# Two RWKV chunks invert their triangular matrices in shared visits, with the first level preset instead of multiplied

## The chip, the cores and the metric

The kernel runs on one core of a Trainium2 chip. The metric is the device time of one launch in microseconds (us); lower is better. All weights start in HBM, so the core reads some 149 MB in one execution.

## The reference

Two transformer blocks over 256 tokens of width 1024, in fp32. The first block has a dilated attention branch and an RWKV-7 branch, merged by gates, then a feed-forward layer; the second has three attention branches, a memory attention and a SwiGLU layer. The change touches only the RWKV-7 branch, which in the reference is a scan over tokens, for 8 heads of width 64:

```python
def step(state, inp):
    r_t, w_t, k_t, v_t, a_t, b_t = inp
    sa = jnp.einsum('bhvk,bhk->bhv', state, a_t)
    state = (state * w_t[:, :, None, :] + sa[..., None] * b_t[:, :, None, :]
             + v_t[..., None] * k_t[:, :, None, :])
    y = jnp.einsum('bhvk,bhk->bhv', state, r_t)
    return state, y
state0 = jnp.zeros((B, RWKV_HEADS, HEAD_DIM, HEAD_DIM), f32)
_, y = lax.scan(step, state0, seq)
```

## The kernel before, in words

**The scan as two chunks.** The 256 tokens are cut into two chunks of 128 (`i` = 0, 1). In a chunk, the tokens' influence on each other is a unit lower triangular 128x128 matrix per head; its inverse is needed. The matrix is cut into two diagonal blocks of 64x64 and the 64x64 block below them (`L21`). `LS` holds the diagonal blocks of all 8 heads, one half of the partitions for each of the two. The inverse of a diagonal block is built by doubling, in six levels `lv` = 0 to 5, from blocks of 1 to blocks of 32: `X` is the inverse so far, kept as `XA` and `XB`, so that each of the two diagonal blocks has it and its transpose. A level has two steps, each of them a visit: **T** multiplies `LS` with `X` on TensorE (PE; 16 products of 64x64x64, lines 1148 and 1151), VectorE (DVE) masks the result out of PSUM into `TL` (line 2851, two instructions, one for each half of the partitions), and **X** multiplies `TL` with `X` (32 products, 24 at level 5, lines 1164 to 1172), which ScalarE (ACT) copies back (through its helper at line 1746) into `XA` and `XB`. At level 0 `X` is a constant identity. After level 5, **S** and **X21** (lines 1183 and 1193, 8 products each) put the block below in place, S read out by DVE and X21 by ACT.

**What stands around the chain.** Ahead of it, `first` makes in four visits the strict products (`LS`, `L21`; lines 1096 and 1099), the received part (`LR`, line 1111) and the keyed parts (`M`, two visits, line 1124). Behind it come `rhs` (line 1214, with 1217 for chunk 1), `u` (1228, 1229) and `y` with the new state `h` (1239 to 1255), and then `normed(i)`, the group norm of a chunk. Chunk 1 goes through `first` and the chain only when chunk 0 has gone all the way to its state.

**The order of the work.** Nothing schedules at run time. Each engine's program is a set of Python generators that run in lockstep; a `yield` ends a *visit*. `turns.mix(fills(), rwkv(), order_1())` interleaves two of them by a string: `m` is a visit of the main work, `s` one of the RWKV side. Main work, which I call *fill*, is the block's input projection: `feature_chunk` for the q and k columns (12 products of 128x128x256 a visit, fp32 weights split in a high and a low part, lines 797, 798, 806) and then `token_range` for the gates (six products of 128x128x512, lines 714 to 716 in `mm3`, a visit). The gates' visits run beside those of `attention` (scores at line 1275, softmax on DVE at 2918 and 2505, its transposes at 720, its output at 1318). `rotate` (line 759) is the rotary embedding of q and k. RWKV's products take PSUM banks 4 to 7 in turn; a bank is free for its next user when the event listed in `free` has come.

**Split.** Each weight slot (1 MB) is split by ACT (1746) and DVE (2574), two instructions each, before PE uses it; three slots take turns.

Of the kernel before, what the change touches and what calls it, by code (L numbers as in the profile page):

```python
# [9 lines left out]
F32R = mybir.dt.float32r  # L10
ALU = mybir.AluOpType
# [32 lines left out]
def shape_constants():  # L44
# [12 lines left out]
    for n in range(7):  # L57
        b = 1 << n
        m = (r // (2 * b) == s // (2 * b)) & (r // b % 2 == 1) & (s // b % 2 == 0)
        if n == 0:  # L60
            c[:, C_M0:C_M0 + 128] = m | (r == s)
        else:
            c[:, C_LV + 128 * (n - 1):C_LV + 128 * n] = m | (r == s)
# [79 lines left out]
class Blank:  # L143
# [13 lines left out]
    tensor_tensor_reduce = max = match_replace = dma_start = matmul  # L157
# [117 lines left out]
def program(nc, A, consts, vecs, pt, out):  # L275
    with ExitStack() as ctx:
# [102 lines left out]
        LS, L21, XA, XB, TL, UA = [view(P + o, 512) for o in (15360, 15872, 17408, 17920, 18432, 19968)]  # L379
# [4 lines left out]
        LS4, L214 = [x.rearrange("p (c w t) -> p c w t", c=4, w=2) for x in (LS, L21)]  # L384
# [163 lines left out]
        def order_1():  # L548
            return itertools.chain("msmsm" * 12, "msmsmsm" * 5, "ms" * 35, "mssss", itertools.cycle("ms"))
# [151 lines left out]
        def tensor_program(e, turns):  # L701
# [291 lines left out]
            def rwkv():  # L993
# [88 lines left out]
                for i in range(2):  # L1082
                    def parts(src, p):
                        return v42(src)[half_rows[p], :, i, :]

                    def first():


                        q.wait_ge(*rw_dve.at("ar", 3))
                        q.wait_ge(*rw_dve.at("b"))  # L1090
                        bs = [next(rw_bank) for _ in range(2)]
                        os_ = [bank(b) for b in bs]
                        for c in range(4):
                            for g in range(2):
                                for p in range(2):
                                    mm(os_[p][half_rows[1 - g], 64 * c:64 * c + 64], parts(A4, p)[:, c, half_rows[g]],
                                       AR[half_rows[p], c, i, 0, half_rows[g]], True, True)
                            for p in range(2):
                                t = mm(os_[p][half_rows[1], 256 + 64 * c:256 + 64 * c + 64], AR[half_rows[p], c, i, 0, half_rows[1]],
                                       parts(A4, p)[:, c, half_rows[0]], True, True)  # L1100
                                if c == 3:
                                    t.then_inc(rw_pe.up("LS", i, p), 1)
                        for p in range(2):
                            free[bs[p]] = [rw_dve.at("L21", i, p)]
                        yield
                        bs = [next(rw_bank) for _ in range(2)]
                        os_ = [bank(b) for b in bs]
                        q.wait_ge(*rw_dve.at("r", 3))
                        for c in range(4):
                            for p in range(2):  # L1110
                                t = mm(os_[p][:, 128 * c:128 * c + 128], parts(A4, p)[:, c, :], AR[half_rows[p], c, i, 1, :], True, True)
                                if c == 3:
                                    t.then_inc(rw_pe.up("LR", i, p), 1)
                        for p in range(2):
                            free[bs[p]] = [rw_dve.at("LR", i, p)]
                        yield
                        q.wait_ge(*rw_dve.at("kt"))
                        for h in range(2):
                            bs = [next(rw_bank) for _ in range(2)]
                            os_ = [bank(b) for b in bs]  # L1120
                            for j in range(2):
                                c = 2 * h + j
                                for p in range(2):
                                    t = mm(os_[p][:, 256 * j:256 * j + 256], parts(KM, p)[:, c, :],
                                           AR[half_rows[p], c, i, :, :].rearrange("p w t -> p (w t)"), True, True)
                                    if j == 1:
                                        t.then_inc(rw_pe.up("M", i, p, h), 1)
                            for p in range(2):
                                free[bs[p]] = [rw_dve.at("M", i, p, h)]
                            yield  # L1130

                    def chain():


                        eye = [const(C_D64, 128)[half_rows[g], 64:128] for g in range(2)]
                        lower, upper = half_rows[1], half_rows[0]
                        for lv in range(6):
                            bs = [next(rw_bank) for _ in range(2)]
                            oA, oB = [bank(b) for b in bs]
                            if lv == 0:  # L1140
                                for p in range(2):
                                    q.wait_ge(*rw_dve.at("ls", i, p))
                            else:
                                for g in range(2):
                                    q.wait_ge(*rw_act.at("x", i, lv - 1, g))
                            for h in range(8):
                                s = slice(64 * h, 64 * h + 64)
# [6 lines left out]
                            for g in range(2):  # L1154
                                free[bs[g]] = [rw_dve.at("T", i, lv, g)]
                            yield
                            bs = [next(rw_bank) for _ in range(2)]
                            oA, oB = [bank(b) for b in bs]
                            for g in range(2):
                                q.wait_ge(*rw_dve.at("T", i, lv, g))  # L1160
                            for h in range(8):
                                s = slice(64 * h, 64 * h + 64)
                                xa, xb = (XA[upper, s], XB[lower, s]) if lv else eye
                                mm(oA[upper, s], TL[upper, s], xa, True, True)
                                t = mm(oB[lower, s], TL[lower, s], xb, True, True)
                                if lv == 5 and h == 7:
                                    t.then_inc(rw_pe.up("X", i, lv, 1), 1)
                                t = mm(oA[lower, s], xa, TL[upper, s], True, True)
                                if h == 7:
                                    t.then_inc(rw_pe.up("X", i, lv, 0), 1)  # L1170
                                if lv < 5:
                                    t = mm(oB[upper, s], xb, TL[lower, s], True, True)
# [4 lines left out]
                            yield  # L1177
                        b = next(rw_bank)
                        o = bank(b)
                        q.wait_ge(*rw_act.at("x", i, 5, 1))  # L1180
                        for h in range(8):
                            s = slice(64 * h, 64 * h + 64)
                            t = mm(o[lower, s], L21[lower, s], XB[lower, s], True, True)
# [2609 lines left out]
```

## Time and profile before

| | before |
|---|---|
| median of 3 runs | 940.78 us (940.57 to 940.81) |
| span of the profiled execution | 938.8 us |
| what lies around the span (median less span) | 2.0 us |
| PE busy | 917.2 us, 98% of the span |
| DVE, ACT, POOL busy | 598.4, 446.8, 43.9 us |
| granted TensorE clock | nine tenths or more in each slice |

No time of its own is recorded for the profiled execution beside its span; it is compared with the median of the runs. The two RWKV chunks' chains, with what feeds them, lie between about 87 and 251 us of the span. A product of two fp32 matrices shows in the trace as two instructions, so 16 products are 32 rows. PE's ends are modelled: consecutive starts tell the rate, not the durations.

### The profile page before, as it was taken

What the parts mean: (1) busy time and instruction counts of PE and PEld (TensorE: products, weight loads), DVE (VectorE), ACT (ScalarE), POOL (GpSimd) and SP (SyncE); (2) the same over time, 40 slices, a digit from 0 to 9 for tenths busy, and PEclk for the clock granted to TensorE, in tenths of its full rate; (3) what the DMA queues carried; (4) which work ended last, traced back from release to release, by engine and by line L of the source; (5) the groups of instructions that cost most, each with busy time, mean ns of one, the idle gap of its engine ahead of it and who ended that gap; (6) DMA issues with size and microseconds to landing.
All of it is one profiled execution on the core that took longest, in us unless ns stands there. A gap on an engine that the chain in (4) does not pass through costs nothing.

```text
span 938.8 us, 15782 instructions
## 1 busy us (share of the span) xinstructions
PE 917.2 (98%) x6760; PEld 771.0 (82%) x6760; DVE 598.4 (64%) x952; ACT 446.8 (48%) x722; POOL 43.9 (5%) x60
## 2 busy tenths in 40 slices
PE   7999999999999999999999999999999999999997
PEld 5999887777889988888889988776778798888885
DVE  4668755764684566655765567877772456666773
ACT  4773344255542444445652446483531345455571
POOL 0010000100000000000000350000000000000000
PEclk9999999999999999999999999999999999999999
DMA  9544332222466766555356774343446556665531
GB/s 331 180 134 137 123 104 91 61 77 91 178 231 206 218 185 196 200 181 184 129 180 156 159 242 138 114 169 123 162 151 199 133 163 192 189 180 181 192 121 45
DMA packets 131205, 150.79 MB, mean 161 GB/s; under 512 B 11808, under 2 KB 102176, under 8 KB 131008
## 3 DMA queue, kind: packets, MB, share of 16 engines
q1 hardware_dynamic: 129920, 145.57, 49.7%
q10 hardware_dynamic: 1216, 4.23, 1.2%
q8 instruction: 53, 0.87, 0.4%
q14 instruction: 16, 0.13, 0.0%
HBM read 148.73 MB, written 1.05 MB: 160 GB/s over the span
## 4 chain that ended last, share of the span: by engine, by line
PE 89%; DVE 6%; ACT 2%; issue 2%; DMA 1%; POOL 0%; POOLq 0%; ACTq 0%
PE psum L825 11%; PE psum L714 9%; PE psum L716 9%; PE psum L715 8%; PE psum L826 6%; PE psum L777 6%; PE psum L797 4%; PE psum L798 4%; PE psum L806 4%; PE psum L720 3%; PE psum L873 3%; PE psum L883 2%; PE psum L874 2%; PE psum L828 2%; PE psum L1643 1%
## 5 line engine op out<-in xcount | busy, mean ns | idle before, releaser
L1746 ACT ACTIVATE parts<-low 128x1024 fp32r<-128x1024 f32 (+3 forms) x246 | 248.6, 1044 | 82.4 <-PE psum L716 60.5
L2574 DVE TENSOR_TENSOR parts<-low,parts 128x1024 fp32r<-128x1024 f32 (+3 forms) x150 | 181.3, 1235 | 22.9 <-ACT parts L1746 22.5
L714 PE MATMUL psum<-parts 128*128 128x512 f32 (+2 forms) x424 | 170.1, 401 | 1.0 <-DVE parts L2574 1.0
L716 PE MATMUL psum<-parts 128*128 128x512 f32 (+2 forms) x424 | 163.6, 386 | 0.0
L715 PE MATMUL psum<-parts 128*128 128x512 f32 (+2 forms) x424 | 163.4, 385 | 0.0
L825 PE MATMUL psum<-parts 128*128 128x512 f32 x434 | 155.6, 398 | 0.0
L1746 ACT ACTIVATE high<-psum 128x512 f32<-128x512 f32 (+4 forms) x102 | 55.8, 564 | 161.7 <-PE psum L828 73.1
L826 PE MATMUL psum<-parts 128*128 128x256 f32 x496 | 129.1, 281 | 0.0
L826 PEld LDWEIGHTS psum<-parts 128*128 128x128 f32 x496 | 93.6, 189 | 5.7
L714 PEld LDWEIGHTS psum<-parts 128*128 128x128 f32 x424 | 79.6, 188 | 21.2 <-issue 2.7
L825 PEld LDWEIGHTS psum<-parts 128*128 128x128 f32 x434 | 81.7, 188 | 16.9
L716 PEld LDWEIGHTS psum<-parts 128*128 128x128 f32 x424 | 79.6, 188 | 16.3
L715 PEld LDWEIGHTS psum<-parts 128*128 128x128 f32 x424 | 79.8, 188 | 14.3 <-issue 0.5
L2637 DVE TENSOR_TENSOR parts<-low,parts 128x1024 fp32r<-128x1024 f32 x54 | 66.0, 1223 | 35.2 <-ACT parts L1746 35.2
L797 PE MATMUL psum<-parts 128*128 128x256 f32 (+2 forms) x296 | 78.0, 299 | 0.0
L798 PE MATMUL psum<-parts 128*128 128x256 f32 (+2 forms) x296 | 73.0, 282 | 0.0
L797 PEld LDWEIGHTS psum<-parts 128*128 128x128 f32 (+2 forms) x296 | 55.7, 188 | 4.1 <-issue 2.9
L777 PE MATMUL psum<-low 128*128 128x128 f32 x512 | 58.2, 275 | 0.4 <-DVE low L2551 0.4
L777 PEld LDWEIGHTS psum<-low 128*128 128x128 f32 x512 | 57.8, 192 | 0.8 <-issue 0.6
L798 PEld LDWEIGHTS psum<-parts 128*128 128x128 f32 (+2 forms) x296 | 55.9, 189 | 1.3 <-issue 1.3
L3031 DVE TENSOR_TENSOR mid<-psum,high 128x512 f32<-128x512 f32 x31 | 21.4, 692 | 44.7 <-ACT high L1746 44.7
L806 PE MATMUL psum<-parts 128*128 128x256 f32 (+2 forms) x296 | 41.4, 282 | 0.0
(318 smaller groups left out, 1356.4 us busy)
## 6 DMA issues: line engine op xcount, KB each, us to landing
low<-in_w_in_dram SPq DMA_DIRECT2D x40, 1024.0 KB, 5.2
low<-in_w_ffn_in_dram SPq DMA_DIRECT2D x44, 512.0 KB, 5.2
low<-in_w_ff_in_dram SPq DMA_DIRECT2D x16, 1024.0 KB, 5.6
low<-in_w_ff_out_dram SPq DMA_DIRECT2D x16, 1024.0 KB, 4.9
low<-in_w_ffn_out_dram SPq DMA_DIRECT2D x11, 1024.0 KB, 5.0
low<-in_w_out_dram SPq DMA_DIRECT2D x8, 1024.0 KB, 5.2
low<-in_w_ple_gate_dram SPq DMA_DIRECT2D x4, 1024.0 KB, 4.9
low<-consts_dram ACTq DMA_DIRECT2D x1, 2142.0 KB, 9.1
```

Source lines behind the costliest of these rows:

```text
L714: mm(o, l[0], r[0], start, False)
L715: mm(o, l[0], r[1], False, False)
L716: return mm(o, l[1], r[0], False, stop)
L777: t = mm(PSUM[0:m, banks[n], 256 * j + 128 * i:256 * j + 128 * i + 128], w3[:, k, off:off + m], uT[:, k, 128 * i:128 * i + 128], k == 0, k ...
L797: mm(o, hi[:, k, c], st.uh[:, k, :], k == 0, False)
L798: mm(o, lo_[:, k, c], st.uh[:, k, :], False, False)
L806: t = mm(o, hi[:, k, c], st.ul[:, k, :], False, k == 7)
L825: mm(p, hi[:, k, c], st.u2(k), k == 0, False)
L826: mm(p[:, 0:256], lo_[:, k, c], st.uh[:, k, :], False, False)
L1746: return e.activation(o, a, ACT.Copy)
L2574: tt(rslot3(n, nk, width)[:, r, 0:w], slot3(n, nk, width)[:, r, 0:w], st.hi3(j)[:, r, 0:w].bitcast(F32), ALU.subtract) \
L2637: tt(rview(OR + 2048 * n + 1024 * (k % 2), 1024), slot(n)[:, 1024 * (k % 2):1024 * (k % 2) + 1024], rview(base, 1024).bitcast(F32), ALU.su ...
```

## The change

Both chunks take each step in the same visit. Every tile of the chain (`LS`, `L21`, `XA`, `XB`, `TL`, `UA`) gets a second copy. In T, chunk 0's products go to the upper and lower halves as before and chunk 1's to the opposite halves of the same two banks, so that one visit holds 32 products. X's visit holds chunk 0's 32 products and then chunk 1's. S and X21 are shared too. Level 0 is no longer multiplied: `strict` computes the 64x64 blocks both ways round (64 products in one visit), ACT presets `LS`, `XA` and `XB` of both chunks with identities (six new copies), and DVE writes the strict triangle and the first subdiagonal over them with `COPY_PREDICATED` (12 instructions, where `first` had 12 of other kinds), then the transposed first superdiagonal with four multiplications by a mask. The block below is made by its own 16 products, at level 4. Chunk 0's received and keyed products and masks move into the T visits of levels 1 to 3; chunk 1's come after chunk 0's state. `order_1` gives the side fewer turns and the fill more.

```diff
-            return itertools.chain("msmsm" * 12, "msmsmsm" * 5, "ms" * 35, "mssss", itertools.cycle("ms"))
+            return itertools.chain("msmsm" * 12, "msmsmms", "mms" * 10, "ms" * 4, "mms" * 7, "ms", "mms" * 6, "m" * 14, itertools.cycle("ms"))
...
+                def strict():
+
+                    q.wait_ge(*rw_dve.at("ar", 3))
+                    q.wait_ge(*rw_dve.at("b"))
+                    bs = [[next(rw_bank) for _ in range(2)] for _ in range(2)]
+                    os_ = [[bank(b) for b in x] for x in bs]
+                    for i in range(2):
+                        for c in range(4):
+                            for w in range(2):
+                                for g in range(2):
+                                    for p in range(2):
+                                        l, r = parts(A4, p, i)[:, c, half_rows[g]], AR[half_rows[p], c, i, 0, half_rows[g]]
+                                        if w:
+                                            l, r = r, l
+                                        o = 256 * w + 64 * c
+                                        t = mm(os_[i][p][half_rows[1 - g], o:o + 64], l, r, True, True)
...
-                        for lv in range(6):
+                    for lv in range(1, 6):
                         bs = [next(rw_bank) for _ in range(2)]
-                        oA, oB = [bank(b) for b in bs]
+                        oL, oU = [bank(b) for b in bs]
...
-                                t = mm(oA[upper, s], LS[lower, s], XA[lower, s] if lv else eye[1], True, True)
+                            for i in range(2):
+                                t = mm(oL[half_rows[i], s], LS[i][lower, s], XA[i][lower, s], True, True)
...
-                                t = mm(oB[lower, s], LS[upper, s], XB[upper, s] if lv else eye[0], True, True)
+                                t = mm(oU[half_rows[1 - i], s], LS[i][upper, s], XB[i][upper, s], True, True)
...
+                            free[bs[g]] = [rw_dve.at("T", i, lv, g) for i in range(2)]
+                        if lv == 1:
+                            received(0)
+                        elif lv < 4:
+                            keyed(0, lv - 2)
+                        elif lv == 4:
+                            below()
                         yield
+                        for i in range(2):
...
+                    for h in range(8):
+                        s = slice(64 * h, 64 * h + 64)
+                        for i in range(2):
+                            t = mm(o[half_rows[1 - i], s], L21[i][lower, s], XB[i][lower, s], True, True)
+                    t.then_inc(rw_pe.up("S"), 1)
...
+                yield from strict()
+                yield from turned()
+                yield from chain()
+                yield from state(0)
+                yield from turns.paired(second(), normed(0))
...
+                def eye(name, i, x):
+                    copy(h8(x), rep(const(C_D64 + 64, 64), 8)).then_inc(rw_act.up("eye", name, i), 1)
...
+                    for i in range(2):
+                        for p in range(2):
+                            o = bank(next(rw_bank))
+                            q.wait_ge(*rw_pe.at("LS", i, p))
+                            e.copy_predicated(LS4[i][:, :, p, :], rep(below, 4).bitcast(I32), quarters(o[:, 0:256])).then_inc(rw_dve.up("ls", i, p), 1)
+                            for n, (x, r) in enumerate(((XA4[i], lower), (XB4[i], upper))):
+                                e.copy_predicated(x[r, :, p, :], rep(first_sub[r], 4).bitcast(I32), quarters(o[r, 256:512])) \
+                                    .then_inc(rw_dve.up("xl", i, p, n), 1)
+                    for i in range(2):
+                        q.wait_ge(*rw_dve.at("ls", i, 1))
+                        for g, (x, r, w) in enumerate(((XA[i], lower, upper), (XB[i], upper, lower))):
+                            tt(h8(x[w]), h8(LS[i][r]), rep(first_sup[r], 8), ALU.mult).then_inc(rw_dve.up("xu", i, g), 1)
```

Counted over PE's program from the strict products to the last gate product, the fill of 288 and 192 products in `feature_chunk` and `mm3`, with the 72 of the up projections behind it, stands in 48 pieces before and in 39 after; a piece is fill that nothing else interrupts.

PE, at the end of the first T visit. Before, it holds lines 1148 and 1151, for one chunk, and fill follows (lines 797 to 806):

```order
L1151 MATMUL psum<-low,high 64x64
L1148 MATMUL psum<-low,high 64x64
L1151 MATMUL psum<-low,high 64x64
L797 MATMUL psum<-parts 128x256
L798 MATMUL psum<-parts 128x256
```

Now lines 1165 and 1168 hold both chunks (chunk 1's `XA` lies in `mid`), line 1118 is `received`, and lines 800 and 801 are the fill:

```order
L1168 MATMUL psum<-high 64x64
L1165 MATMUL psum<-mid,high 64x64
L1168 MATMUL psum<-high 64x64
L1118 MATMUL psum<-high 128x128 x8
L800 MATMUL psum<-parts 128x256
L801 MATMUL psum<-parts 128x256
```

The received products, which had a visit of their own ahead of the chain, now stand behind the two chunks' T products.

DVE, after the strict products, now. Lines 2901 and 2903 are the predicated copies, 2908 the superdiagonals, 2747, 2714 and 2753 the rotary embedding, 2643 a slot's split, 2939 the masks of T (before: 2851), 2915 the mask of `received`:

```order
L2903 COPY_PREDICATED mid<-low,psum 64x4x64
L2903 COPY_PREDICATED high<-low,psum 64x4x64
L2908 TENSOR_TENSOR high<-high,low 64x512 x2
L2908 TENSOR_TENSOR mid<-high,low 64x512
L2908 TENSOR_TENSOR high<-high,low 64x512
L2747 TENSOR_TENSOR mid<-psum,low 128x512
L2714 TENSOR_TENSOR mid<-psum,low 128x512
L2753 TENSOR_TENSOR mid<-mid 128x512
L2643 TENSOR_TENSOR parts<-low,parts 128x1024 x2
L2747 TENSOR_TENSOR mid<-psum,low 128x512
L2939 TENSOR_TENSOR high<-psum,low 64x512 x4
L2915 TENSOR_TENSOR high<-psum,low 128x4x128 x2
```

All that `strict` gives DVE now stands in one run ahead of the next slot's split, and the first four T masks come behind that split.

DVE at the third attention block's softmax (lines 2918, 2925 and 2505). Before, T's masks (2851), two operations of `normed(0)` (2816, 2818) and a split (2574) stand between its maxima and its scaling:

```order
L2918 ISA low 128x1
L2851 TENSOR_TENSOR high<-psum,low 64x512 x2
L2816 TENSOR_TENSOR high<-high 128x4x128
L2818 TENSOR_TENSOR high<-high 128x4x128
L2574 TENSOR_TENSOR parts<-low,parts 128x1024
L2925 RECIPROCAL low<-low 128x1
L2505 TENSOR_SCALAR mid<-mid,low 128x768
```

Now it is `rhs`'s copy for chunk 1 (2961), a variance (2873, and a small 2574) and the split (2643), ahead of the scaling (3030, 2574):

```order
L3023 ISA low 128x1
L2961 COPY high<-psum 128x512
L2873 TENSOR_REDUCE low<-high 128x8
L2574 TENSOR_SCALAR low<-low 128x8
L2643 TENSOR_TENSOR parts<-low,parts 128x1024
L3030 RECIPROCAL low<-low 128x1
L2574 TENSOR_SCALAR mid<-mid,low 128x768
```

The chain's masks are gone from the last three softmaxes: the chain is over before the second attention block.

## Rows read from the trace of the kernel before

**Rows 1.** The page: span, busy time of each engine, granted clock in 40 slices.

```profile
span 938.8 us, 15782 instructions
PE 917.2 (98%) x6760; PEld 771.0 (82%) x6760; DVE 598.4 (64%) x952; ACT 446.8 (48%) x722; POOL 43.9 (5%) x60
PEclk9999999999999999999999999999999999999999
```

**Rows 2.** Windows: length, busy us of each engine, clock, DMA share, GB/s.

```profile
110.00:145.00 35.00, 34.77 (x649) 30.86 (x649) 20.92 (x26) 12.92 (x20) 0.00 (x0) 1.00 0.30 92
145.00:172.00 27.00, 25.98 (x366) 20.58 (x365) 12.95 (x22) 9.80 (x17) 0.00 (x0) 1.00 0.26 79
172.00:251.00 79.00, 74.33 (x1132) 58.49 (x1129) 48.55 (x87) 39.29 (x69) 3.88 (x2) 1.00 0.28 95
```

**Rows 3.** Timeline of PE, a T visit, `rotate`, an X visit: start, duration.

```profile
110.76 0.27 PE L1148 MATMUL psum<-low,high 64*64 64x64 f32 x1
...
110.86 0.22 PE L1148 MATMUL psum<-low,high 64*64 64x64 f32 x1
...
110.92 0.22 PE L1148 MATMUL psum<-low,high 64*64 64x64 f32 x1
...
111.83 0.39 PE L797 MATMUL psum<-parts 128*128 128x256 f32 x1
...
114.81 1.02 PE L759 MATMUL psum<-mid,low 128*128 128x512 f32 x2
115.77 0.27 PE L1164 MATMUL psum<-low,high 64*64 64x64 f32 x1
...
116.86 0.38 PE L797 MATMUL psum<-parts 128*128 128x256 f32 x1
```

**Rows 4.** The chain of waits, 90 to 250 us: start, us, what.

```profile
97.78 0.31 PE psum L797
...
99.39 1.06 PE psum L1124 x8
...
157.74 1.14 PE psum L1193 x16
158.88 0.43 PE psum L714
159.54 0.24 PE psum L716
160.47 0.33 PE psum L720 x3
160.80 1.08 PE psum L1214 x32
161.88 0.43 PE psum L714
```

**Rows 5.** Timeline of DVE during the third attention block.

```profile
193.10 0.69 DVE L2918 CUSTOM_DVE_ANT_0 mid<-psum,low 128x512 f32<-128x512 f32 x1 [3.70 <-PE psum L1275]
...
195.39 1.40 DVE L2851 TENSOR_TENSOR high<-psum,low 64x512 f32<-64x512 f32 x2
196.82 0.69 DVE L2816 TENSOR_TENSOR high<-high 128x512 f32<-128x512 f32 x1
...
198.16 1.22 DVE L2574 TENSOR_TENSOR parts<-low,parts 128x1024 fp32r<-128x1024 f32 x1
199.29 0.15 DVE L2925 RECIPROCAL low<-low 128x1 f32<-128x1 f32 x1
199.48 0.62 DVE L2505 TENSOR_SCALAR mid<-mid,low 128x768 f32<-128x768 f32 x1
```

**Rows 6.** Timeline of PE in the same block; in brackets its idle time.

```profile
196.94 0.24 PE L1164 MATMUL psum<-high 64*64 64x64 f32 x1 [1.10 <-DVE high L2851]
```

**Rows 7.** Groups by line and shape, DVE: count, busy us, mean ns, idle.

```profile
L2851 DVE TENSOR_TENSOR high<-psum,low 64x512 f32<-64x512 f32 x24 | 16.5, 688 | 12.9 <-PE psum L1151 12.5
L2826 DVE TENSOR_TENSOR high<-psum,low 128x256 f32<-128x256 f32 x4 | 1.7, 425 | 2.3 <-PE psum L1099 2.2
L2714 DVE TENSOR_TENSOR_SCAN high<-high 128x1024 f32<-128x1024 f32 x1 | 2.3, 2284 | 0.0
```

**Rows 8.** Timeline of ACT after the strict products' operands; in brackets its idle time.

```profile
85.96 2.00 ACT L1746 ACTIVATE parts<-low 128x1024 fp32r<-128x1024 f32 x2
94.42 0.60 ACT L1746 ACTIVATE mid<-psum 128x512 f32<-128x512 f32 x1 [6.46 <-PE psum L806]
```

**Rows 9.** Timeline of DVE: the first mask of `first`, chunk 0.

```profile
92.78 0.42 DVE L2826 TENSOR_TENSOR high<-psum,low 128x256 f32<-128x256 f32 x1 [2.19 <-PE psum L1099]
```

**Rows 10.** Groups by line and shape, ACT, 80 to 250 us.

```profile
L1746 ACT ACTIVATE high<-psum 128x512 f32<-128x512 f32 x26 | 14.4, 596 | 29.3 <-PE psum L1172 18.8 <-PE psum L1244 6.9 <-PE psum L720 3.6
```

More of the change, by code:

```diff
@@ L1194, in chain @@
[L1194 to L1203 removed]
+                    for h in range(8):
+                        s = slice(64 * h, 64 * h + 64)
+                        for i in range(2):
+                            t = mm(o[half_rows[i], s], XA[i][lower, s], TL[i][lower, s], True, True)
@@ L2819, in normed, with strict @@
                     yield
-                for i in range(2):
-                    def first():
+                upper, lower = half_rows
+                def strict():
+                    below, first_sub, first_sup = [const(o, 64) for o in (C_D64, C_M0, C_M0 + 64)]
+                    for name in ("A", "B", "S"):
+                        for i in range(2):
+                            q.wait_ge(*rw_act.at("eye", name, i))
+                    for i in range(2):
                         for p in range(2):
@@ new lines, in strict, with received, keyed @@
+                    yield
+                def received(i):
+                    for p in range(2):
+                        o = bank(next(rw_bank))
+                        q.wait_ge(*rw_pe.at("LR", i, p))
+                        tt(LR4[:, :, p, :], quarters(o), rep(const(C_IU, 128), 4), ALU.mult).then_inc(rw_dve.up("LR", i, p), 1)
+                def keyed(i, h):
+                    msk = const(C_SU, 256).unsqueeze(1).broadcast_to([128, 2, 256])
+                    for p in range(2):
+                        o = bank(next(rw_bank))
+                        q.wait_ge(*rw_pe.at("M", i, p, h))
+                        tt(halves(MN[p][:, 512 * h:512 * h + 512]), halves(o), msk, ALU.mult).then_inc(rw_dve.up("M", i, p, h), 1)
@@ L2862, in rwkv @@
-                    if i == 0:
-                        yield from first()
-                        yield from turned()
-                        yield from chain()
-                    else:
-                        yield from turns.paired(itertools.chain(first(), chain()), normed(0))
+                    o = bank(next(rw_bank))
+                    q.wait_ge(*rw_pe.at("S"))
+                    for i in range(2):
+                        e.tensor_copy(TL[i][lower], o[half_rows[1 - i]]).then_inc(rw_dve.up("S", i), 1)
@@ L2885, in rwkv, with second @@
                     yield
+                def second():
+                    received(1)
+                    keyed(1, 0)
+                    yield
+                    keyed(1, 1)
+                    yield
+                    yield from state(1)
+                yield from strict()
+                yield from turned()
+                yield from chain()
+                yield from state(0)
+                yield from turns.paired(second(), normed(0))
                 yield from normed(1)
```

336 lines of the change are left out of this document (173 added, 163 removed).

## The prediction

> **What bounds the kernel now.** I read the page first: PE is busy for 98% of the span and no other engine for more than 64%, at the full granted clock throughout [rows 1]. So PE's own time sets the end, and a change counts by the PE time that it takes away and by the gaps that it closes or opens. The windows over the stretch of the two chains show those gaps: PE idles for 35.00 − 34.77 = 0.2 us, 1.0 us and 4.7 us in three windows, 5.9 us in all [rows 2]. DVE, at 50 to 60% there, is the engine behind most of them. Everything behind 251 us is untouched, and what is won before it should move the rest forward as it stands.
>
> **How small products are paid.** The timeline of PE gives a price for a visit, not for a product. A T visit (16 products, 32 instructions) starts at 110.76 and the next work at 111.83: 1.07 us. An X visit has twice as many and takes 115.77 to 116.86: 1.09 us [rows 3]. Successive instructions of one line start 0.06 us apart (110.86, 110.92). T's two lines use two 64x64 quarters of the array and X's four lines all four, so a visit costs 16 steps of 0.059 us, 0.94 us, and 0.14 us to get going, however many quarters work. X21, 16 instructions in one quarter, takes 1.14 us in the chain of waits (157.74 to 158.88) [rows 4]. T therefore leaves half of the array empty, S and X21 three quarters; that is what sharing visits can use.
>
> **The change, part by part** (PE, us).
> - T: 12 visits at 1.07 become 5, with 64 instructions on four quarters as X has: 5 x 1.09 = 5.45 for 12.84. −7.4, of which level 0 is 2.1.
> - X: its quarters are full already, so pairing saves only the start: a pair is 32 steps, 1.89 + 0.14 = 2.03. Five pairs are 10.15 for 12 x 1.09 = 13.08. −2.9, of which level 0 is 2.2.
> - S and X21: four visits at 1.07 (1.14 less the overlap with the next work) become two. −2.1.
> - `strict`: 128 instructions on four quarters are 32 steps, 2.03, for two `first` visits at 1.08: −0.1. The block below: 8 steps and a start, +0.6. The received and keyed products keep their number and, having another shape, their start. Together +0.5.
> - Fill restarts: the first instruction of a piece takes 0.43 us in the chain where a later one takes 0.24 (158.88, 159.54), and 0.31 for a 256-column one that then runs at 0.12. That is 0.2 a piece, and there are 39 pieces for 48: −1.8.
> - Gaps. Two of 1.1 us (one shown) stand in front of X in the third and fourth attention block: T's masks end late on DVE behind four softmax instructions [rows 5, 6]. The chain is over by then in the new order, and these and the chain's other waits go. Before X there are now about 5.2 us of PE work (received or keyed 1.07, a piece of fill 1.6 (97.78 to 99.39) [rows 4], `rotate` 0.96 (114.81 to 115.77) [rows 3], another 1.6) where one piece stood; the four masks take 4 x 0.7 = 2.8 us [rows 7]. Before the next T there are 3.0 us of fill, for four ACT copies of 0.6 us [rows 10] of which two are left when X ends. What stays late is the softmax: in the third block DVE has maxima 2.3, a copy 0.7, a variance 0.9, a split 1.2 and a scaling 0.8, 5.9 us, and PE has 2.0 + 3.0 = 5.0 us in between, so about 1 us of idleness. In the fourth PE has 3.4 us and DVE 3.1 plus ACT's exponential between them: 0.2. At the first T masks (next paragraph) about 0.3. 1.5 us for 5.9: −4.4, of which I take 4.0 since the other transposes of attention may wait too.
>
> **DVE after the strict products.** The trace has no predicated copy. Its cheapest price is that of the multiplication it replaces, 0.43 us for 256 columns [rows 7]. The dearest is the slowest streaming instruction in the trace, the scan with 2284 ns for 1024 columns, 0.57 for 256 and with 0.15 of fixed cost about 0.75 us [rows 7]. It is a masked copy of the same shape as the multiplication, so I take 0.45. Then the 12 copies and four superdiagonals occupy DVE from 92.8, when the first products are there [rows 9], for 5.4 + 2.8 us to 101.0; three rotary operations at 0.7 and the split of the next slot (two at 1.2) end near 105.5. On PE `strict` ends at 93.6, and two long pieces of fill (3.0 each), a short one (1.5), `rotate` and eight transposes (0.8) put the first T at 102.9 and the end of its visit at 105.0. The next fill needs that split's second half about 105.9, and X needs the four masks at 105.0 + 1.6 + 0.96 + 1.6 = 109.1, when DVE ends them (a rotary operation 0.7 and 4 x 0.7 behind 105.5) at about 109.0. So this fits with less than 0.5 us to spare, and the cover is PE's own fill. At 0.75 each, DVE is 3.6 us later and PE waits for about 3.5: that is the upper bound. Nothing cheaper than 0.43 is in sight for the shape, and a cheaper one would gain nothing, the work being hidden. The six identity copies on ACT (6 x 0.6 = 3.6 us) fall into its 6.46 us of idleness between 88 and 94.4 [rows 8] and are in front of one split only, whose slot is not read for another 5 us. Without that cover they would be worth the 3.6. In all other places DVE and ACT have about as much to do as before: 20 T masks for 24, four more copies for the block below.
>
> **The sum.** −7.4 − 2.9 − 2.1 + 0.5 − 1.8 − 4.0 = −17.7. The profiled span of 938.8 becomes 921.1; with the 2.0 between span and median, 923.1. The median of the runs shown is 940.78, and I give 923.
>
> **A rule against it.** The rows show that two column halves over the same rows run side by side: `rhs`, 32 instructions of 128 rows by 64 columns, takes 1.08 us (160.80 to 161.88) [rows 4], and X's four quarters 1.09. The Trainium skill (TensorE: Matmul & The Clock Gate, Part 3: Packing small matmuls) says that weight loads overlap running products only when the row group differs. By that rule S and X21, whose two chunks share the lower rows, would stay at two times 16 steps each. The trace does not agree for pairs of other shapes. This gives one of the rivals below.
>
> **The rivals.**
> - *Quarters do not share.* For it: chunk 0's and 1's products in T, S and X21 share row halves, and no row shows just this pairing. Against it: the rows above. Price: T 5 x 0.94 = 4.7 and S and X21 1.9, so 923.1 + 6.6 = 929.7. If only S and X21 fail, by the skill's rule, 925.0. Chance 0.05.
> - *DVE falls behind.* For it: predicated copies near the upper bound, or masks, rotary operations and split in one in-order queue, with a bank that X's first half now gets only when both chunks' masks are done. Against it: DVE is busy 60% there [rows 2]. Price: 3.5 at the start, 1 to 4 more in later levels and softmaxes: 926 to 931, about 928. Chance 0.15.
> - *More is won*: no gap stays and the softmaxes fit too: 918 to 920. Chance 0.06.
> - *Nothing comes out*: the fill, now denser, waits for its weights and gives the time back: about 940. Against it: the DMA share is 0.3 [rows 2]. Chance 0.02.
> - *Slower*: a predicated copy that takes several passes. With some 0.5 us to spare, each further 0.1 us on the 12 costs 1.2; at 1.9 us each the loss is 17 and the gain is gone, and at 2.2 us the time is 923 + 12 x 1.75 − 0.5 = 943.5. No row has anything like it: it would be 8 ns a column against the scan's 2.2. Chance 0.02.
> - *As forecast*: 920 to 926. Chance 0.70.
>
> **Numbers.** The likeliest case gives 923. The range from 918.5 to 929.5 takes in the forecast, most of the extra gain, the upper bound of the predicated copy and most of the lag of DVE; about 0.1 is left out on each side or less. What this measurement can tell from no change is 0.2%, 1.9 us. Faster takes in all cases but two: 0.96; same 0.02; slower 0.02.
>
> **What the changed profile would show.** PE's instructions fewer by 128; T visits of 64 instructions with the next work 1.09 us after their start, X pairs 2.03 us, S and X21 1.07 each; COPY_PREDICATED at about 0.45; PE's idleness from 87 us to the last gate product 1 to 3 us; the up projections about 18 us earlier, and every later stage as long as it was. I am wrong if T takes 2 us, if a predicated copy takes over 0.75, if a gap opens in front of the first two X pairs, or if the saved time reappears as waits for splits in the gates' last seven visits, which now stand in one piece.

## The result, and the profile after

The changed kernel takes 926.12 us (median of four, 924.88 to 926.23) against 940.67 us for the kernel before, measured beside it (940.29 to 940.81). The ratio is 0.9844, with a 95% interval of 0.9832 to 0.9855: faster by 14.6 us. The forecast was 923.0 with a range of 918.5 to 929.5. The profiled execution took 926.23 us, 924.4 of it span, so its span is 14.4 us shorter than that in [rows 1]. One execution of one experiment below, the wait put back, took 1119.87 us at a mean granted clock of 0.75 and counts in no median.

The page and the windows of the changed kernel (columns as in [rows 2]; the last window holds the up products and the transposes behind them):

```profile
span 924.4 us, 15532 instructions
PE 903.4 (98%) x6632; PEld 761.9 (82%) x6632; DVE 598.1 (65%) x956; ACT 447.6 (48%) x724; POOL 44.4 (5%) x61
```

```profile
110.00:145.00 35.00, 34.89 (x844) 31.28 (x845) 27.33 (x39) 15.29 (x25) 0.00 (x0) 1.00 0.29 93
145.00:172.00 27.00, 26.22 (x407) 21.30 (x407) 15.33 (x25) 12.55 (x22) 0.00 (x0) 1.00 0.25 79
172.00:234.00 62.00, 59.01 (x580) 47.20 (x579) 37.75 (x70) 29.91 (x53) 5.03 (x2) 0.97 0.33 105
234.00:256.00 22.00, 20.29 (x92) 15.72 (x91) 19.53 (x25) 11.92 (x17) 0.00 (x0) 1.00 0.57 209
```

PE has 128 instructions fewer and is still what sets the end. Its idle time is not gone: 0.11, 0.78, 2.99 and 1.71 us in these windows, and 5.74 us from 87 to 270 us where the kernel before had 6.28 in the same stretch. One granted clock is no longer 1.00: 0.97 between 172 and 234 us.

The timeline of PE shows the new visits; the start of a visit and the start of the work behind it are what to compare with [rows 3, 4]: the first T visit with the received products behind it, an X pair, S, X21.

```profile
102.52 0.27 PE L1165 MATMUL psum<-high 64*64 64x64 f32 x1
...
103.61 1.16 PE L1118 MATMUL psum<-high 64*128 64x128 f32 x16
104.70 0.38 PE L800 MATMUL psum<-parts 128*128 128x256 f32 x1
...
120.16 0.27 PE L1190 MATMUL psum<-high 64*64 64x64 f32 x1
...
122.19 0.39 PE L800 MATMUL psum<-parts 128*128 128x256 f32 x1
...
159.29 0.27 PE L1212 MATMUL psum<-high 64*64 64x64 f32 x1
...
160.37 0.50 PE L717 MATMUL psum<-parts 128*128 128x512 f32 x1
...
162.28 0.27 PE L1224 MATMUL psum<-high 64*64 64x64 f32 x1
...
163.36 0.50 PE L717 MATMUL psum<-parts 128*128 128x512 f32 x1
```

T with 64 instructions takes 1.09 us, the X pair 2.03, S and X21 1.08 each.

The predicated copies, one line of DVE's queue by source line (in ns: shortest, median, longest):

```profile
L2903 DVE COPY_PREDICATED high<-low,psum x6: 436/444/452, 93.2 to 97.5; 64x256 f32<-64x256 int32 x6
L2901 DVE COPY_PREDICATED high<-low,psum x4: 426/429/445, 92.7 to 96.6; 128x256 f32<-128x256 int32 x4
```

What PE waited for from 87 to 256 us (total us, times, longest), in the view of the waits:

```profile
PE psum L723 <- DVE low L3023: 2.4, 1, 2.4
PE psum L723 <- DVE mid L2577: 0.9, 1, 0.9
PE psum L1315 <- DVE mid L2753: 0.8, 1, 0.8
PE psum L723 <- DVE mid L2574: 0.6, 1, 0.6
PE psum L1378 <- ACT mid L1782: 0.4, 1, 0.4
PE psum L876 <- ACT parts L1782: 0.3, 1, 0.3
PE psum L1190 <- DVE high L2915: 0.2, 1, 0.2
```

The waits in front of X are gone, all but 0.2 us. The two largest waits are new. The largest stands in front of the four transposes of `normed(0)`; this is PE's timeline around it:

```profile
209.06 1.67 PE L1315 MATMUL psum<-mid 64*128 64x256 f32 x12
213.08 0.72 PE L723 MATMUL psum<-low,high 128*128 128x128 f32 x4 [2.35 <-DVE low L3023]
213.50 0.73 PE L717 MATMUL psum<-parts 128*128 128x512 f32 x1
214.03 0.63 PE L718 MATMUL psum<-parts 128*128 128x512 f32 x1
214.46 0.63 PE L719 MATMUL psum<-parts 128*128 128x512 f32 x1
...
216.59 0.57 PE L718 MATMUL psum<-parts 128*128 128x512 f32 x1
217.00 0.39 PE L719 MATMUL psum<-parts 128*128 128x512 f32 x1
```

L3023 is the softmax's maximum over the scores. The transposes read nothing of it. What they share with it is PSUM bank 4: RWKV's ring is (4, 5, 6, 7), attention's is (2, 3, 4), and in the new order the ring of RWKV comes to 4 just when the scores of the fourth attention block (209.06) have taken it. And there is a second cost: behind the wait, products of 512 columns start 0.43 us apart (214.03, 214.46) instead of 0.23 (217.00 and the next, at 217.23). In windows of 2 us the granted clock reads:

```profile
210.00:212.00 2.00, 0.73 (x7) 0.33 (x4) 1.30 (x5) 0.08 (x1) 0.00 (x0) 1.00 0.82 212
212.00:214.00 2.00, 0.92 (x5) 0.86 (x6) 1.73 (x6) 1.89 (x5) 0.00 (x0) 0.89 0.81 312
214.00:216.00 2.00, 2.00 (x6) 1.58 (x5) 0.79 (x2) 2.00 (x7) 0.00 (x0) 0.50 0.00 0
216.00:218.00 2.00, 2.00 (x8) 1.50 (x8) 1.54 (x2) 1.38 (x2) 0.00 (x0) 0.76 0.00 0
218.00:220.00 2.00, 2.00 (x14) 1.70 (x13) 1.97 (x3) 1.36 (x3) 0.00 (x0) 1.00 0.00 0
```

A clock of 0.50 is the 1.2 GHz level. Between 213.50 and 217.00 eight products were started in 3.50 us. At 0.23 apart, with 0.08 more for the first, they need 1.9, so the slow clock cost 1.6 us.

The second largest wait stands behind the up products, in front of the next transposes:

```profile
253.73 1.06 PE L723 MATMUL psum<-low,high 128*128 128x128 f32 x8 [0.87 <-DVE mid L2577]
255.14 0.47 PE L876 MATMUL psum<-parts 128*128 128x512 f32 x1 [0.34 <-ACT parts L1782]
```

The kernel before has only the 0.34 there. By the program this is a shared bank again: these transposes take banks 5 and 6, and in the new order the fourth and last of RWKV's up products has bank 5, which they can have only when DVE has read it (L2577).

The idle time and the slow clock leave the work. The span fell by 14.4, idleness by 0.5, and the slow clock added 1.6, so PE's own work fell by 15.5 us.

### The profile page after: what moved, and what is told of

Read it like the earlier page. It is cut to its first block, busy times and chain, and to the rows that moved or that the text cites. A ratio compares the mean times of both kernels' runs of the same rounds, so it can differ in the third digit from the quotient of the medians.

```text
span 924.4 us, 15532 instructions
## 1 busy us (share of the span) xinstructions
PE 903.4 (98%) x6632; PEld 761.9 (82%) x6632; DVE 598.1 (65%) x956; ACT 447.6 (48%) x724; POOL 44.4 (5%) x61
## 4 chain that ended last, share of the span: by engine, by line
PE 87%; DVE 7%; ACT 2%; issue 2%; DMA 1%; POOL 0%; POOLq 0%; ACTq 0%; DVEq 0%
PE psum L828 11%; PE psum L717 9%; PE psum L718 9%; PE psum L719 9%; PE psum L829 6%; PE psum L780 6%; PE psum L800 4%; PE psum L801 3%; PE psum L809 3%; PE psum L723 3%; PE psum L876 3%; PE psum L877 2%; PE psum L886 2%; PE psum L831 2%; PE psum L1683 1%
## 5 line engine op out<-in xcount | busy, mean ns | idle before, releaser
L1786 ACT ACTIVATE high<-psum 128x512 f32<-128x512 f32 (+5 forms) x93 | 51.3, 563 | 150.6 <-PE psum L831 72.7
L800 PE MATMUL psum<-parts 128*128 128x256 f32 (+2 forms) x296 | 78.8, 302 | 0.0
L801 PE MATMUL psum<-parts 128*128 128x256 f32 (+2 forms) x296 | 72.8, 282 | 0.0
L3580 POOL TENSOR_TENSOR low<-low 128x1 f32<-128x1 f32 x20 | 11.0, 552 | 640.0 <-DVE low L2574 563.3
```

The lines of the kernel that those rows point to most:

```text
L800: mm(o, hi[:, k, c], st.uh[:, k, :], k == 0, False)
L801: mm(o, lo_[:, k, c], st.uh[:, k, :], False, False)
L1786: return e.activation(o, a, ACT.Copy)
```

## The experiments

Each was timed in rounds with the kernel before, whose median was 940.58 to 940.77 in all of them. Differences between two experiments are differences of their medians. In code, PE's program is shown; ACT and DVE are changed to match.

**Level 0 alone** (on the kernel before). In PE's chain:

```diff
-for lv in range(6):
+yield
+yield
+for lv in range(1, 6):
...
-    t = mm(oA[upper, s], LS[lower, s], XA[lower, s] if lv else eye[1], True, True)
+    t = mm(oA[upper, s], LS[lower, s], XA[lower, s] if lv > 1 else eye[1], True, True)
```

> The kernel before, without level 0 of each chunk's chain: its T and X visits, their masks and copies are left out and level 1 starts from the identity, while the two turns stay, empty (so the chain's result isn't the inverse, and the output isn't the reference's). It prices level 0 alone. Theory: each chunk loses a T visit (1.07 us), an X visit (1.09) and two restarts of a product behind them (0.2 each), 2.56 us, in sum 5.1 us, and some of the short waits around them, 0.5 to 1: 940.7 - 5.7 = 935.0 us (934.3 to 936.2). Rival: the empty turns pull the next steps together, so that VectorE and ScalarE come late for level 1 and the gain falls to 3 us or less (937.7 or more).

It took 935.44 us, ratio 0.9945 (0.9930 to 0.9960): −5.1 us. The windows from 87 to 270 us hold 6.27 us of idleness against 6.28 before, so all of it is work: two T visits (2.14), two X visits (2.18) and four restarts at 0.2 (0.8) are 5.1. The further 0.5 to 1 us that I had expected from short waits did not come; the rival's 3 us neither. Level 0 is about a third of the change.

**Quarters one pair at a time** (on the changed kernel). In the T visit, and likewise in S and X21:

```diff
-for h in range(8):
-    s = slice(64 * h, 64 * h + 64)
-    for i in range(2):
+for i in range(2):
+    for h in range(8):
+        s = slice(64 * h, 64 * h + 64)
         t = mm(oL[half_rows[i], s], LS[i][lower, s], XA[i][lower, s], True, True)
```

> The changed kernel with the two chunks' products in the T, S and X21 visits one chunk after the other, 32 (16) instructions in the same quarters of the array and then 32 (16) in the other, instead of in turn. Theory: what makes a T visit of 64 instructions as short as one of 32 (1.09 us) is that four different quarters are addressed in turn; with two quarters at a time each T visit takes 2 x 1.07 = 2.14 us (+1.05, five times: +5.3) and S and X21 2 x 1.07 each (+1.06, twice: +2.1), in sum +7.4, less what waits take up: 926.1 + 7.4 = 933.5 us (931 to 934). Rival: the order doesn't matter, the queue of the engine finds the free quarter by itself: T visits stay at 1.1 us and the time at 926.

930.33 us, ratio 0.9887 (0.9872 to 0.9902): 4.2 us more than the changed kernel. In its timeline of PE the same T visit begins at 102.77, chunk 1's half of it at 103.53 and the received products at 104.61:

```profile
102.77 0.27 PE L1165 MATMUL psum<-high 64*64 64x64 f32 x1
...
103.53 0.27 PE L1165 MATMUL psum<-mid,high 64*64 64x64 f32 x1
...
104.61 0.49 PE L1118 MATMUL psum<-high 64*128 64x128 f32 x4
```

1.84 us instead of 1.09. My 2.14 was 0.30 too high: the second half begins 0.76 us behind the first and not 1.07, while the first's last products are still being started. S (161.95 to 163.78) and X21 (165.69 to 167.51) are longer by as much. 0.75 us in each of five T visits, S and X21 are 5.3 us; of these 1.1 were absorbed by waits that shrank (idleness from 87 to 270 us is 4.63 us for 5.74). So the quarters' sharing is real, it depends on the order in which the instructions are written, and it is worth some 4 to 5 us here.

**One piece of cover instead of two** (on the changed kernel):

```diff
-"mms" * 10, "ms" * 4, "mms" * 7, "ms", "mms" * 6, "m" * 14
+"ms" * 28, "m" * 37
```

> The changed kernel with the same steps in another order: from the first paired step on one piece of the other products stands between any two steps of the chunks (28 times), and the 37 pieces that are left come behind, where the change has two pieces between most steps and 14 behind. Theory: two pieces are needed to cover the doubled masks (4 x 0.7 us) and copies (4 x 0.6 us) of a paired step; with one piece of 1.4 to 2.9 us the matrix engine waits 0.5 to 1.3 us at each of some 20 steps, +8 to +20 us, so 934 to 946 us. Rival: one piece covers them (what stands in a piece is long enough), the time is within 2 us of 926.

931.25 us, ratio 0.9899 (0.9883 to 0.9916): 5.1 us more than the changed kernel. PE waits in front of X as the theory has it, at the first levels:

```profile
108.61 0.24 PE L1190 MATMUL psum<-high 64*64 64x64 f32 x1 [1.37 <-DVE high L2939]
109.93 0.24 PE L1190 MATMUL psum<-mid,high 64*64 64x64 f32 x1 [0.16 <-DVE high L2915]
111.96 0.21 PE L1191 MATMUL psum<-high 64*64 64x64 f32 x1 [1.27 <-issue]
```

Idleness from 87 to 145 us is 5.8 us for 0.3, far from the 8 to 20 us expected: most steps with one piece are covered. Against it stand the later windows: 2.32 us of idleness between 172 and 234 us instead of 2.99, and a clock of 1.00 there. The direction was right, the size too high: 5.1 us for 8 at the least. Nor is all of it waiting. The span is 4.6 us longer; from 87 to 270 us idleness is 9.97 us for 5.74, and the slow clock gives back its 1.6, so 2.0 us are PE's work, which these rows do not explain.

**Another bank for the transposes** (on the changed kernel). In `normed`:

```diff
+if i == 0:
+    next(rw_bank)
 b = next(rw_bank)
 o = bank(b)
 q.wait_ge(*rw_dve.at("yc", i))
```

> The changed kernel with one thing other: the transposes of normed(0) take the next bank of the ring (5) in place of bank 4, which the attention ring shares. Theory: the wait of 2.35 us before these transposes at 213.08 is a wait for bank 4, which had just been given to the scores of the fourth attention block, and the low granted clock that follows (0.50 at 214 to 216 us) costs some 1.5 us more; both go, so the kernel takes 926.1 - 3.9 = 922.2 us (921.5 to 923), and no slice near there has a granted clock under 0.9. Rival A: the transposes wait for the normalised rows of VectorE and not for the bank: the wait stays, 926 us. Rival B: the low clock has nothing to do with the wait: 2.35 us are won (923.8), and the slow stretch stays. Rival C: the bank behind it collides in its turn: a new wait at the next rows of the state, 924 to 926.

The extra `next` also moves everything behind it in RWKV's ring on by one bank. 922.90 us, ratio 0.9812 (0.9797 to 0.9827): 3.2 us less than the changed kernel (by the profiled spans 3.8), with the clock at 1.00 in every window. The transposes now start 1.60 us behind the scores, with no wait. A smaller wait appears behind them:

```profile
209.15 1.67 PE L1317 MATMUL psum<-mid 64*128 64x256 f32 x12
210.75 0.66 PE L723 MATMUL psum<-low,high 128*128 128x128 f32 x4
...
218.00 0.44 PE L723 MATMUL psum<-low,mid 128*128 128x128 f32 x2 [1.35 <-ACT mid L1788]
...
250.98 0.66 PE L723 MATMUL psum<-low,high 128*128 128x128 f32 x4 [0.34 <-DVE mid L2581]
```

The theory's two halves hold, with rival C as a remainder: ACT comes late with the copies of the transposed softmax, since the four scalings of `normed` (1.49 us) and a split (2.01 us) stand ahead of them in its queue. The last row is a gain that the theory did not have: behind the up products PE now waits 0.34 us where it waited 0.87 and 0.34, since the last of them is no longer in bank 5. So 0.87 us of what this edit wins in the profile belong to the second conflict; no run changes that one alone.

**The wait put back, without the bank** (on the last kernel):

```diff
 q.wait_ge(*rw_dve.at("yc", i))
+if i == 0:
+    q.wait_ge(*at_dve.at("r", 1, 1, 1, 1))
```

> e1_bank's kernel (its own bank for the first transposes) with only the wait put back: the same transposes wait until VectorE has made all four reads of the fourth attention block's scores (about 212.9 in the trace of the changed kernel), which is what bank 4 made them wait for. Theory: the price is that of an idle stretch of about 2.3 us, whatever its cause, and the granted clock falls behind it to 0.5 for some 3 us: the time is that of the changed kernel, 926.1 us (925.3 to 926.8). Rival: the low clock in the changed kernel came from something else near it; then only the wait is paid, less the 1.35 us wait at 218.00 that it replaces: 924 us, with a clock of 1.0.

925.37 us, ratio 0.9836 (0.9823 to 0.9850): 2.5 us more than the kernel with the new bank. The wait and the clock are back:

```profile
213.06 0.80 PE L723 MATMUL psum<-low,high 128*128 128x128 f32 x4 [2.44 <-DVE low L3038]
```

```profile
214.00:216.00 2.00, 2.00 (x6) 1.53 (x5) 0.78 (x2) 2.00 (x5) 0.00 (x0) 0.50 0.00 0
```

So it is the wait that counts, whatever it is for. It does not bring back all of the 3.2 us: the time stays 0.75 us under the changed kernel's, the span 1.0. The second conflict, which is still away here (0.34 us at 253.66, no 0.87), is of that size.

**A shorter wait** at the same place, for the third read (`"r", 1, 1, 1, 0`):

> As e7_hold, but the transposes wait only for the third of the four reads (about 212.2), so the idle stretch is some 1.4 us. Theory: after an idle stretch of 1.4 us the granted clock stays at 1.0, as it does in e1_bank behind the wait of 1.35 us at 218.00, and the later wait at 218.00 shrinks by what is waited here: 923 us (922.5 to 923.6). Rival: any wait of over 1 us at this place lowers the clock (the stretch before it is thin in work, 0.66 us of small products after 12 score products): 924.5 to 925.5.

923.13 us, ratio 0.9815 (0.9802 to 0.9829): as without any wait. PE idles 1.65 us there, the clock stays at 1.00, and the wait of 1.35 us behind is gone:

```profile
212.82 0.63 PE L723 MATMUL psum<-low,high 128*128 128x128 f32 x4 [1.65 <-DVE low L3031]
```

```profile
214.00:216.00 2.00, 2.00 (x10) 1.62 (x9) 1.03 (x3) 2.00 (x7) 0.00 (x0) 1.00 0.03 9
```

A wait of 1.65 us was free, because a later one took it up; 0.8 us more cost 2.2.

**The up weights' splits behind the reads** (on the changed kernel). On ACT and DVE the four splits move to the steps of the attention up products, on DVE each behind a read (`next(reads)`, then `up_columns("r", n)`):

> The changed kernel with ScalarE's four splits of the RWKV up weights behind its read of the last gate bank, and VectorE's remainders of them behind its reads of the up products, where now the first two splits stand ahead of the read and wait for the weights' DMA (1.79 us, until 234.49). Theory: the waits of the attention up products (0.44 at 237.03, and 0.3 in sum before 238.59 and 240.32) hang on that late DMA and go: 926.1 - 0.7 = 925.4 us. Rival: the splits come late for the RWKV up products instead, which then wait 1 us or more: 926 to 928.

927.27 us, ratio 0.9855 (0.9841 to 0.9868): no gain; it is 1.1 us more, but the two ratios' intervals overlap. The waits that I wanted to remove went, and the rival's took their place, in the middle of the RWKV up products:

```profile
244.31 0.50 PE L1378 MATMUL psum<-parts 128*128 128x512 f32 x1 [1.95 <-DVE parts L3055]
```

DVE makes the fourth remainder there at 243.04, behind two operations of `normed(1)` and a read.

**Both edits**:

> The changed kernel with both edits: bank 5 for the first transposes (e1_bank, 922.9 us) and the up weights' splits behind the reads (e5_tail). The two places are 20 us apart, so the gains add: 922.9 - 0.7 = 922.2 us; if the splits come late, 923 to 925.

925.06 us, ratio 0.9835 (0.9821 to 0.9848). The wait for the fourth split is again 1.95 us, at 242.37. But in this profile the granted clock behind it is 0.50 from 244 to 246 us, while in the one before it stayed at 1.00 behind the wait of the same length.

**The fourth split earlier** (on the last kernel; the third and fourth go together, `for k in ((0,), (1,), (2, 3), ())[n]`):

> e6_both's kernel with one thing other: the fourth split of the RWKV up weights goes directly behind the third on ScalarE and VectorE, ahead of the last read of the attention up products, for which the matrix engine had waited 1.95 us in e5_tail and e6_both. Theory: with it neither the late DMA nor the late split holds the matrix engine, and the time is e1_bank's less the waits of its tail (0.34 us in the trace at 250.98 and some 0.4 of pauses too short for a row): 922.9 - 0.7 = 922.2 us. Rival: VectorE has no room left there, the third and fourth split push the reads back, and the wait only moves: 923 to 924.5.

923.07 us, ratio 0.9813 (0.9799 to 0.9826). The wait of 1.95 us is gone, so its cause was the split's place. But the rival is right in that the wait moves: VectorE's reads come later, and the transposes behind the up products wait for them, where with the bank alone they wait 0.34 us:

```profile
251.16 0.66 PE L723 MATMUL psum<-low,high 128*128 128x128 f32 x4 [1.19 <-DVE mid L2580]
```

The time is no better than with the new bank alone (922.90). The edit at the weights is worth nothing.

**The transposes one piece earlier** (on the last kernel), in the order:

```diff
-"ms" * 4, "mms" * 7,
+"ms" * 4, "mms" * 5, "msm", "mms",
```

> e9_tail2 with one exchange in the order: the chunks' step with the transposes of normed(0) goes one piece earlier, ahead of the gate products and the scores of the fourth attention block. Theory: ScalarE, idle for 4 us there, then has its four scalings (1.49 us) behind it before the softmax's exponentials, and the wait of 1.35 us at 218.00 for its copies goes too: e9_tail2 less 1.3 us, 921 us. Rival: the normalised rows aren't ready a piece earlier, and the transposes wait for VectorE or GpSimd: e9_tail2's time or more.

921.82 us, ratio 0.9800 (0.9787 to 0.9813): 1.25 us less. The wait for ACT is gone from the profile; between 172 and 234 us only 0.64 us at 195.97 and 0.18 at 214.27 are left, waits for the softmax. The rival fell.

**That exchange alone, bank 4 kept**:

> The changed kernel with that exchange alone, the transposes in bank 4 as in the change. Theory: the bank's conflict turns round, the scores now wait for ScalarE's four scalings to leave bank 4, which it begins some 0.6 us behind the transposes and needs 1.5 us for, while gate products of some 2.8 us stand between them: no wait is left and no low clock, 926.1 - 3.9 - 1.3 = 921 us, so that the order alone is worth as much as bank and order. Rival: bank 4's second user comes too soon, and a wait of 0.5 to 1 us stays: 922 to 923.

923.99 us, ratio 0.9819 (0.9806 to 0.9833). Most of the gain comes, but the conflict turned round leaves small waits, the clock staying at 1.00:

```profile
208.08 0.66 PE L723 MATMUL psum<-low,high 128*128 128x128 f32 x4 [0.38 <-ACT high L1786]
210.34 1.67 PE L1315 MATMUL psum<-mid 64*128 64x256 f32 x12 [0.21 <-ACT high L1782]
...
251.04 1.06 PE L723 MATMUL psum<-low,high 128*128 128x128 f32 x8 [0.87 <-DVE mid L2577]
252.45 0.47 PE L876 MATMUL psum<-parts 128*128 128x512 f32 x1 [0.34 <-ACT parts L1782]
```

The waits of 0.38 and 0.21 are the rival's, in the size that it gave. Its 922 to 923 was 1 us too low, and the theory's 921 by 3. The ring keeps its old phase here, so the second conflict is still there (0.87). These three waits, 1.5 us, are gone in the next kernel, which is 2.1 us shorter; the rest is not explained.

**Bank and exchange**, the version that the others point to:

> The changed kernel with bank 5 for the transposes and the exchange in the order, and the up weights' splits where the change has them. Theory: the splits' place is worth nothing once the earlier wait is gone (e9_tail2 923.1 against e1_bank 922.9), so the time is e10_swap's, 921.8 us or up to 0.3 less, with granted clock 1.0 and no wait over 0.7 us between 172 and 234. Rival: the late DMA of the up weights costs its 0.7 us again, now that the products before it end sooner: 922.5 us.

921.90 us, ratio 0.9799 (0.9786 to 0.9813): 4.2 us less than the changed kernel and 18.9 less than the kernel before. PE waits 0.39 us at 233.80 for ACT's read of the gate bank and 0.34 before the transposes at 250.46; the late weights cost no 0.7 us here either.

## Why the prediction was right, and where it was off

The time, 926.12, is inside the range, and 3.1 us above the number given. By its own steps:

- *What bounds the kernel.* Right. PE is busy for 98% before and after. The work behind the up products moved as a block: from the restart of PE at 255.14 to the end of the span it is 669.3 us, before 669.2.
- *The price of a visit, 0.14 + 16 x 0.059 however many quarters work.* Right: T 1.09 (1.09 forecast), the X pair 2.03 (2.03), S and X21 1.08 (1.07), `strict` 2.02 (2.03). The experiment with the quarters one pair at a time shows that the sharing is the cause. The rival that they don't share had 6.6 us as its price; 5.3 us were measured in rows, 4.2 in the time.
- *The Trainium skill's rule (TensorE: Matmul & The Clock Gate, Part 3)*, that weight loads overlap running products only when the row group differs, would have left S and X21 at twice 16 steps. In S all instructions contract over the lower rows, and 32 of them took 1.08 us. For these shapes the trace does not agree with it.
- *Level 0, 2.1 of T and 2.2 of X, with restarts at 0.2.* Right: 5.1 us measured, 5.1 by these terms.
- *The predicated copy, 0.45.* Right: 0.43 to 0.45. The start of the chain had no wait but 0.2 us in front of the first X, so DVE's work there was hidden as worked out.
- *Work in all*: −13.7 forecast, −15.5 measured. For 0.9 of the difference there is a row pattern: `rotate` with the piece behind it took 2.39 us (106.23 to 108.62), where [rows 3, 4] give 0.96 + 1.6. Now a piece of fill follows it directly in all five places, where small products or transposes did. The rest isn't resolved.
- *Gaps, 5.9 us to 1.5, taken as −4.0.* This is the step that failed. Idleness fell by 0.5 us only. Of its parts, the waits in front of X went and the softmax of the third block waits 0.63 us (1 forecast). The sentence that failed is the one on the fourth block, "PE has 3.4 us and DVE 3.1 plus ACT's exponential between them: 0.2": I counted the work between two dependent steps and not the buffers. The new order gave bank 4 to the scores just before the transposes asked for it, for 2.35 us. It also gave bank 5 to the last up product just before the next transposes asked for that one, for 0.87 us. The slow clock of 1.6 us was in no term at all. The wait of 0.78 us before the first scores, where DVE has the last rotary operation behind four T masks (148.69 to 151.5), wasn't foreseen either.
- *Waits for splits in the gates' last seven visits*, named as a way to be wrong, did not come; the up projections behind them had 1.7 us of waits in sum. In the same window they were 0.55 us with the bank changed and nothing done for the weights, 0.87 of the difference being the second conflict.

By the profiled spans the forecast is 3.3 us too low (921.1 for 924.4), and that is a sum of errors with both signs: 3.5 us of gaps that stayed and 1.6 of slow clock, against 1.8 us of work that went beyond the forecast. That the kernel with the changed bank takes the forecast's 923 (922.90) is in part luck too: its work fell by the same 15.5 us where 13.7 were forecast, and it still idles 3.5 us from 87 to 270 us where the forecast left 1.5.

The wait at bank 4 is shown as a cause: the edit that takes it away gives 3.2 us, and the wait put back alone takes 2.5. That 1.6 of them are the clock's is read from the starts in one execution. The remaining 0.7 has the size of the second conflict's 0.87, whose wait stands in the profiles of all five kernels with the old phase of the ring and in none with the new; it was not tried by itself.

## What to carry to other kernels

When steps of two streams are reordered, walk through the buffers that the streams share as well as through the data that they wait for: here two PSUM banks that came to two users at the wrong time took 3.2 us of a gain that is 17.7 us without them, most of it (2.5) one bank. Price small products by visits (a start and the steps of the busiest quarter), and write instructions for different quarters in turn. Before moving work out of the way of a small wait, see who waits for it next: the splits moved behind the reads opened a wait of 1.95 us to close waits of 0.7.

## What the runs showed of the hardware that I had not expected

A wait of PE of some 2.4 us in front of the first transposes (2.35 in the changed kernel and in the one with only the weights' splits moved, 2.44 where it was put back) was followed by about 3 us at half the granted clock (0.50), and products of 512 columns then started 0.43 us apart instead of 0.23. Behind 1.35 and 1.65 us it stayed at 1.00. A wait of 1.95 us did either: 1.00 behind the one at 244.31, 0.50 behind the one at 242.37 of another kernel. What decides there was not settled. The times may show the same: the kernels with waits of 1.95 us or more scatter by 1.4 to 3.1 us (the changed kernel 924.88 to 926.23, both edits 923.46 to 926.60), the one with the bank changed by 0.6 and the one with the fourth split earlier by 0.11. It isn't the only source of scatter, since the exchange alone scatters by 1.9 (923.21 to 925.14) with a clock of 1.00 in the slowest of its executions.

The other: the order of writing decides whether quarters share. The same 64 instructions took 1.09 us with four quarters in turn and 1.84 us with two at a time.
